# Expert down projection: loads of seven neighbouring rows per partition, and the hidden columns reordered to match

## The reference

```python
def swiglu(x, w_gate, w_up, w_down):
    return (jax.nn.silu(x @ w_gate) * (x @ w_up)) @ w_down

def moe_ffn(x, w_router, b_router, w_gate, w_up, w_down):
    ...
    for e in range(N_EXPERTS):
        out = out + gates[..., e:e + 1].astype(x.dtype) * swiglu(x, w_gate[e], w_up[e], w_down[e])
    return out
```

## Time and profile before

| | |
|---|---|
| median of 3 runs | 1052.32 us (1050.55 to 1055.87) |
| the profiled execution, its own time | 1050.54 us |
| its span, first to last instruction | 1048.8 us |
| TensorE busy | 1007.4 us, 96% |
| TensorE weight loads busy | 905.9 us, 86% |
| VectorE busy | 746.8 us, 71% |
| ScalarE busy | 634.7 us, 61% |
| moved by DMA | 287.16 MB, mean 274 GB/s |
| the chain that ended last | TensorE 53%, DMA 19%, VectorE 14%, ScalarE 8% |

### The profile page before, as it was taken

The page is one execution under the profiler, slowest core; times in us unless marked ns, Lnnn a source line. Parts: engine busy times, 40 slices in busy tenths (PEclk is TensorE's granted clock), DMA queues, the critical chain, the costliest instruction groups (busy, mean ns, idle before and its releaser), DMA issues.

```text
span 1048.8 us, 14406 instructions
## 1 busy us (share of the span) xinstructions
PE 1007.4 (96%) x5588; PEld 905.9 (86%) x5588; DVE 746.8 (71%) x730; ACT 634.7 (61%) x667; POOL 39.8 (4%) x62
## 2 busy tenths in 40 slices
PE   7999999999999999999799999999999999999985
PEld 6987889999999998888698888888888888898874
DVE  4557565555556647765667879888897879888877
ACT  5655444434444546454566777878777787777763
POOL 1201000000000000000020000000000000000110
PEclk9999999999999999999789999999999999999998
DMA  9744588787664665235459999999999999999991
GB/s 322 221 144 141 204 278 284 241 243 250 200 221 146 206 173 155 81 140 178 164 202 394 343 368 390 356 378 359 376 377 367 367 350 385 358 386 375 370 395 65
DMA packets 144954, 287.16 MB, mean 274 GB/s; under 512 B 10001, under 2 KB 65313, under 8 KB 144914
## 3 DMA queue, kind: packets, MB, share of 16 engines
q1 hardware_dynamic: 142338, 277.63, 75.2%
q0 software_dynamic: 2576, 8.97, 2.4%
HBM read 269.81 MB, written 16.78 MB: 273 GB/s over the span
## 4 chain that ended last, share of the span: by engine, by line
PE 53%; DMA 19%; DVE 14%; ACT 8%; issue 5%; POOL 1%; DVEq 0%; ACTq 0%; SPq 0%; POOLq 0%
PE A L478 14%; PE A L480 13%; PE A L479 13%; DMA raw<-in_moe_w_up 9%; DVE lo L1319 9%; DMA raw<-in_moe_w_down 7%; ACT hi L945 5%; PE S L478 2%; PE S L480 2%; PE S L479 2%; DMA raw<-in_moe_w_gate 2%; PE T L523 2%; DMA raw<-in_gm_w_in 1%; PE T L558 1%; PE T L831 1%
## 5 line engine op out<-in xcount | busy, mean ns | idle before, releaser
L1319 DVE TENSOR_TENSOR lo<-raw,hi 128x1792 fp32r<-128x1792 f32 (+3 forms) x320 | 556.0, 1779 | 157.4 <-ACT hi L945 156.2
L945 ACT ACTIVATE hi<-raw 128x1792 fp32r<-128x1792 f32 (+3 forms) x320 | 464.8, 1504 | 201.8 <-PE A L480 101.7
L478 PE MATMUL A<-lo,xT_hi 128*128 128x448 f32 (+2 forms) x964 | 352.9, 366 | 10.0 <-DVE lo L1319 7.5
L479 PE MATMUL A<-hi,xT_lo 128*128 128x448 f32 (+2 forms) x964 | 347.0, 360 | 0.0
L480 PE MATMUL A<-hi,xT_hi 128*128 128x448 f32 (+2 forms) x964 | 347.0, 360 | 0.0
L478 PEld LDWEIGHTS A<-lo,xT_hi 128*128 128x128 f32 x964 | 181.8, 189 | 33.1 <-DVE lo L1319 14.7
L480 PEld LDWEIGHTS A<-hi,xT_hi 128*128 128x128 f32 x964 | 181.8, 189 | 16.0
L479 PEld LDWEIGHTS A<-hi,xT_lo 128*128 128x128 f32 x964 | 182.0, 189 | 14.4
L478 PE MATMUL S<-lo,xT_hi 128*128 128x512 f32 x224 | 89.8, 401 | 3.8 <-DVE lo L1319 3.5
L480 PE MATMUL S<-hi,xT_hi 128*128 128x512 f32 x224 | 87.5, 391 | 0.0
L479 PE MATMUL S<-hi,xT_lo 128*128 128x512 f32 x224 | 87.3, 390 | 0.0
(11 more groups left out here) (213 smaller groups left out, 861.5 us busy)
## 6 DMA issues: line engine op xcount, KB each, us to landing
raw<-in_moe_w_gate SPq DMA_DIRECT2D x32, 1792.0 KB, 9.2
raw<-in_moe_w_up SPq DMA_DIRECT2D x32, 1792.0 KB, 9.4
raw<-in_moe_w_down SPq DMA_DIRECT2D x32, 1792.0 KB, 9.6
raw<-in_ff_w_gate SPq DMA_DIRECT2D x8, 1408.0 KB, 6.9
raw<-in_ff_w_up SPq DMA_DIRECT2D x8, 1408.0 KB, 6.9
raw<-in_ff_w_down SPq DMA_DIRECT2D x8, 1408.0 KB, 6.6
raw<-in_gm_w_in SPq DMA_DIRECT2D x10, 1024.0 KB, 5.2
slots<-sel SPq DMA_DIRECT2D x18, 512.0 KB, 8.0
```

The source lines that it names most:

```text
L478: nc.tensor.matmul(out, stat[0], mov[1], start=start, stop=False)
L479: nc.tensor.matmul(out, stat[1], mov[0], start=False, stop=False)
L945: return nc.scalar.activation(out, in_, ACT.Copy)
L1319: nc.vector.tensor_tensor(piece(lo, SPLIT, u, i), piece(raw, RAW, u, i), piece(hi, SPLIT, u, i).bitcast(F32), ALU.subtract).then_inc(lo_do ...
```

## The change

A down unit no longer holds a column half of seven spread-out row blocks. The 896 rows of a hidden half are dealt to the partitions in runs of seven: partition `p` takes rows `7p` to `7p+6`, whole, which is one run of 28 KB in memory. The first unit of a pair carries the first 14 KB of each run (rows 0, 1, 2 and the first half of row 3), the second the rest. The block `k` of the sum is now the rows `7p + k`, so the hidden columns must come in the same order: VectorE's multiply writes column `7i + k` to place `k*128 + i`.

Each down unit now adds to both banks of S, so TensorE waits for both before unit 8, and both are complete only after unit 11; `output_rows` and `output_hi` wait for that. The second unit of a pair runs its seven products in a new order.

```diff
             def expert_loads(e, ve):
 ...
-                        w, k0, c0 = moe_w_down, 7 * ((j - 8) // 2), 512 * (j % 2)
-                    src = w[0, bass.ds(e, 1), k0 * P:(k0 + k) * P, c0:c0 + n]
 ...
+                        c, i = divmod(j - 8, 2)
+                        src = moe_w_down[0, bass.ds(e, 1), c * ECH:(c + 1) * ECH, :]
+                        sp.dma_start(raw[:, at:at + UNIT],
+                                     src.rearrange("e (p k) n -> p (e k n)", p=P)[:, i * UNIT:(i + 1) * UNIT]
+                                     ).then_inc(raw_full[u % RAW], 16)
 ...
-            def down(ve, u, c, half):
-                s = S_MOE + 2 + c
-                bank = S[s % 2]
-                if half == 0:
-                    pe.wait_ge(s_free[s % 2], ve * (PER_S // 2) + s // 2)
-                for kk in range(7):
-                    split_ready(u, kk, ve)
-                    k = 7 * half + kk
-                    last = three(bank[:, :], [a[:, k * P:(k + 1) * P] for a in hT],
-                                 (part(hi, u, kk, 0, 512), part(lo, u, kk, 0, 512)), k == 0, k == EB - 1)
+            def down(ve, i):
+
+                u, c, second = U_MOE + 8 + i, i // 2, i % 2
+                if i == 0:
+                    for s in (S_MOE + 2, S_MOE + 3):
+                        pe.wait_ge(s_free[s % 2], ve * (PER_S // 2) + s // 2)
+                half = UNIT // 2
+                products = [(k, n) for k in range(4) for n in range(2)][:7]
+                if second:
+                    products = [(4, 0), (5, 0), (3, 1), (4, 1), (6, 0), (5, 1), (6, 1)]
+                pe.wait_ge(lo_done, ve * (2 * MU) + 2 * u + 1)
+                early = True
+                for k, n in products:
+                    at = k * D + n * 512 - second * UNIT
+                    if early and at + 512 > half:
+                        pe.wait_ge(lo_done, ve * (2 * MU) + 2 * u + 2)
+                        early = False
+                    ring = (u % SPLIT) * UNIT + at
+                    kk = 7 * c + k
+                    last = three(S[(S_MOE + n) % 2][:, :], [a[:, kk * P:(kk + 1) * P] for a in hT],
+                                 [r[:, ring:ring + 512] for r in (hi, lo)], kk == 0, kk == EB - 1)
                 last.then_inc(used, 1)
 ...
             def output_rows(c, ve):
 
-                act.wait_ge(used, ve * MU + U_MOE - 1 + c)
+                act.wait_ge(used, ve * MU + U_MOE)
 ...
             def output_hi(c):
 
-                act.wait_ge(used, rounds * MU + U_MOE - 1 + c)
+                act.wait_ge(used, rounds * MU + U_MOE)
 ...
                 for b in range(2):
-                    cols = slice(b * EN, (b + 1) * EN)
-                    nc.vector.tensor_tensor(ehid[:, cols], A[ju % 2][b][:, 0:EN], esilu[:, cols],
+                    cols, lines = slice(b * EN, (b + 1) * EN), slice(b * EN // 7, (b + 1) * EN // 7)
+                    by_k = ehid.rearrange("p (k i) -> p i k", k=7)[:, lines, :]
+                    nc.vector.tensor_tensor(by_k, A[ju % 2][b][:, 0:EN].rearrange("p (i k) -> p i k", k=7),
+                                            esilu[:, cols].rearrange("p (i k) -> p i k", k=7),
                                             ALU.mult).then_inc(a_free[ju % 2], 1)
```

More of the change, by code:

```diff
@@ L411, in expert_loads @@
                     u = U_MOE + j
-                    k, n = moe_shape[j]
+                    at = (u % RAW) * UNIT
+                    sp.wait_ge(lo_done, ve * (2 * MU) + 2 * (u - RAW) + 2)
                     if j < 8:
@@ L415, in expert_loads @@
                         k0, c0 = 4 * (j % 2), ECH * (j // 4)
-                    else:
-                        w, k0, c0 = moe_w_down, 7 * ((j - 8) // 2), 512 * (j % 2)
-                    src = w[0, bass.ds(e, 1), k0 * P:(k0 + k) * P, c0:c0 + n]
[L419 to L423, removed]
+                        src = w[0, bass.ds(e, 1), k0 * P:(k0 + 4) * P, c0:c0 + ECH]
+                        sp.dma_start(raw[:, at:at + UNIT].rearrange("p (k n) -> p k n", n=ECH),
+                                     src.rearrange("e (k p) n -> p (e k) n", p=P)
+                                     ).then_inc(raw_full[u % RAW], 16)
+                    else:
+                        c, i = divmod(j - 8, 2)
+                        src = moe_w_down[0, bass.ds(e, 1), c * ECH:(c + 1) * ECH, :]
+                        sp.dma_start(raw[:, at:at + UNIT],
+                                     src.rearrange("e (p k) n -> p (e k n)", p=P)[:, i * UNIT:(i + 1) * UNIT]
+                                     ).then_inc(raw_full[u % RAW], 16)
                     if j == 5:
@@ L927, in _ @@
                 emptied_T(t1 + 1)
-                down(ve, U + 8, 0, 0)
+                down(ve, 0)
                 hidden_T_expert(ve, 1, t1 + 2)
-                down(ve, U + 9, 1, 0)
+                down(ve, 1)
                 emptied_T(t1 + 2)
                 emptied_T(t1 + 3)
-                down(ve, U + 10, 0, 1)
+                down(ve, 2)
                 with pe.If(ve < rounds - 1):
                     turn_rows(t1 + 4, ve)
-                down(ve, U + 11, 1, 1)
+                down(ve, 3)
             pe.wait_ge(selT_set, 1)
```

## The result

The changed kernel took 1056.48 us (median of 20 runs, 1053.31 to 1060.66); the kernel before, run beside it, 1052.88 (20 runs). The medians stand 3.6 us apart; the ratio of the runs is 1.0025, 95% interval [1.0013, 1.0037], which is 2.6 us (1.4 to 3.9). By either number the kernel is slower, where I had forecast 5.3 us less. The text goes by ratios, since all experiments have one. The profiled execution has a span of 1054.1 us.

The account below looks back on a forecast made before the run. TensorE and DMA were both taken as nearly full. Six middle rounds at -0.57 us gave -3.4, the last round -1.5; with its gate part and rounding -5.3 us, so 1047.0 us from a median of 1052.32, range 1038 to 1059.

Parts of the forecast that it names:

- Packets: Down loads: 14 KB runs instead of 2 KB packets save 0.5 us a load, landing in 8.6 to 9.2 us.
- the line: DMA packet time taken as 11.6 ns a packet plus 0.0357 ns a byte, giving 523 ns for 14 KB.
- Down products, third load: TensorE's wait at load 10 goes because that load lands 1.0 to 1.5 us sooner: -0.77 us a round.
- Gate and up products: Waits at the fourth and fifth load shrink as the next expert's loads are issued sooner: -0.3 us a round.
- Second load of a pair: Down products: load 9 needs its second half sooner, adding a wait of +0.5 us a round; load 11 costs nothing.
- Strided writes: VectorE's four multiplies a round, writing with a 512 B step, stay at 615 ns: no cost.
- the first rival: VectorE's strided write is slow: 0.93 us more a pair, 11.2 us over eight rounds, 1058.2 us; chance 0.23.
- The high end: Upper bound for VectorE's strided multiply, doubling the part that grows with length: 1.08 us a multiply.
- Last round, output copies: Loads 8 and 11 shorten the last round by 1.5 us; waiting for both banks and later output copies cost nothing.

Follow-up runs that it names:

- R: Long runs: down loads as 128 runs of 14 KB; alone in the kernel before 1051.01 us, 0.9970; fitted part -2.3 us.
- The light version: Kernel before without the down products' matmul of hidden low part with high weights, 28 matmuls a round: 1050.94 us, 0.9978.
- O: Product order in which loads 9 and 11 need their second half after one product; alone in the kernel before 1054.37 us, 1.0004.
- S: VectorE's strided multiply write; alone in the kernel before 1054.05 us, 1.0016; fitted part +2.4 us.

## Why the prediction was wrong

**Packets.** Right in kind, a little too good in size: the runs were not cut up, and 419 GB/s is 4.38 us a load, 0.36 saved where I took 0.5; by the packets of all six rounds (90.1 and 577.8 ns, the line had said 523) it is 0.4. The 8.9 us to landing lay inside 8.6 to 9.2, with some luck: two of the nine kernels with long runs show 9.5 and 9.6. The rule of the Trainium skill (DMA: Bandwidth & Descriptors, Specifications), by which there was nothing to gain above 512 B, does not hold here by 387 against 419 GB/s and by R's -2.3 us.

**Down products, third load.** Right: the wait at load 10 went (0.7 us are left in S products with long runs alone).

**Gate and up products.** Wrong, and the costliest step. I had -0.3 us a round here and none of the gain given back. With long runs alone these waits grew from 8.5 to 11.6 us, +0.5 a round. I costed each wait by itself, as if removing one left the others where they were, and wrote that "that is the most a faster supply can give back", without asking what TensorE would wait for next. With this term and the packets together I had long runs at -0.77 - 0.3 a round and -1.8 for the last round and rounding, some 8 us; they measured 2.3. This error alone turns the forecast's sign: with 2.3 in place of 8 and all else as forecast the sum is slightly above the kernel before. The light version points to why: supply and TensorE were both within 1 us of a round's length, so either one's gain stops at the other.

**Second load of a pair.** Right in kind: the wait at load 9 is there in all six rounds. I had 0.5 us a round and the profile has 0.92. The strided pair ahead of it is not the reason: with the plain write the wait is 1.07 a round, and 1.0 where O stands alone. Yet O costs +1.9 us in all against my +3.0, since a part of this wait only stands in for others (at load 10 they went from 4.2 us in six rounds to 0.2 with O alone).

**Strided writes.** Wrong: I took 0 and it is +0.38 us a multiply and +2.4 us in all. The reason that I gave, that the multiply "went by the number of elements and not by where they lie", compared two rows that both walk in single runs; it could not speak about steps. The rule of the Trainium skill that I put beside the first rival stood against it and was right for this step. The high end (1.08 us) held the 995 ns, and a multiply above 0.8 us was one of the signs of being wrong that I had named.

**The first rival** gave 1058.2, and 1056.48 looks like it. Its mechanism was there, its price was not: it put 11.2 us on the stride, and 2.4 were measured. Even with the measured 0.38 us its way of counting, 24 times in all, would give 9.1 us, where 2.4 us is six times. That its time comes near is luck: it took the gain of long runs too large by 6 us and the stride's price too large by 9.

**Last round, output copies.** The copies and the two banks cost nothing to be seen (1050.86 us with them, 1051.01 without). The 1.5 us that I gave the last round are not told apart by any run; in that round TensorE's granted clock was 1.00 before and is 0.97 in the changed kernel's profile, where 3.4 us from 1015.63 run at half clock (1.2 GHz) after 10.6 us in which TensorE was busy for 7.4. So the two rows of that round do not compare.

The sum by measured parts: R -2.3, S +2.4, O +1.9, together +2.0 us, against +2.6 measured (1.0025).

## What to carry to other kernels

Before removing a wait, take the work away from the engine that waits: if leaving out 51 us of matmuls buys 2 us, a wait removed there is likely to reappear at the next thing the supply delivers, and gains are to be costed against both resources and not wait by wait. When a permutation has to be put somewhere, look which side lies in PSUM or moves two elements per 16 bytes of SBUF; the same permutation cost 0.38 us an instruction on VectorE's SBUF side and nothing on its PSUM side. And a change with several parts can hide a good one: long runs with the step on the PSUM side and the products in lying order took 1051.79 us (0.9980 of before, [0.9964, 0.9997]), some 4.7 us less than the kernel with all three parts, whose interval [1.0013, 1.0037] it does not touch. Against the kernel before the gain is 0.2%, and its interval only just leaves out no change.

## What I had not expected of the hardware

- VectorE's multiply on fp32 pays 0.8 ns per element when its SBUF side, read or write, has one element in 16 bytes (962 to 978 ns for 448 elements at 16 B, 975 at 64 B, 995 at 512 B), and nothing at two (616 to 619 ns at 8 B). A step of 28 B costs somewhat more than one of 512 B (1059 against 995 in the write); why is open, and so is where between 8 and 16 B the price begins.
- PSUM reads with a step of 28 B are free for VectorE's multiply and ScalarE's silu (614 and 535 ns, against 615 and 536).
- TensorE's weight load of 128 x 128 fp32 with a step of 28 B takes 210 ns instead of 140.
- Runs of 14 KB move faster than packets of 2 KB, 419 GB/s against 387 in a stretch of one kind and 397 against 364 by the mean packet of six rounds. A down load lands in 8.7 to 9.6 us with them and in 9.4 to 9.6 without; the gate and up loads between them land no sooner (9.7 us after the change, 9.2 and 9.4 before).
